# First FFN chunk of each layer: the two tiles' first products by turns, four sums made earlier on VectorE, weight sums in place

## What is computed

```python
def swiglu_ffn(h, w_gu, w_down):
    gate, up = jnp.split(h @ w_gu, 2, axis=-1)
    return (jax.nn.silu(gate) * up) @ w_down
...
x = x + swiglu_ffn(rms_norm(x, ffn_norm[layer]), ffn_w_gu[layer], ffn_w_down[layer])
```

## Time and profile before

| what | value |
|---|---|
| median of 3 runs | 2767.73 us (2766.87 to 2770.54) |
| profiled execution | 2769.94 us, span 2768.1 us |
| TensorE matmul busy | 2699.3 us, 98% of the span |
| VectorE / ScalarE / GpSimd busy | 1355.6 / 826.3 / 1263.7 us |
| chain that ended last | TensorE 91%, VectorE 5%, ScalarE 2% |
| mean granted TensorE clock | 0.994 |

### The profile page before, as it was taken

How to read it: one execution, slowest core, us unless ns; L and a number is a source line. 1 busy time by engine, 2 the same in 40 slices (tenths; PEclk the granted TensorE clock), 3 DMA queues, 4 the chain that set the end, 5 groups by cost and what they waited for, 6 DMA issues and landing times.

```text
span 2768.1 us, 35757 instructions
## 1 busy us (share of the span) xinstructions
PE 2699.3 (98%) x12145; PEld 2236.5 (81%) x12145; DVE 1355.6 (49%) x1866; ACT 826.3 (30%) x1404; POOL 1263.7 (46%) x1215
## 2 busy tenths in 40 slices
PE   7999999999999899999999999999988999999998
PEld 6888888888888788888888788787876888888886
DVE  7423423432334764454545537355577454545555
ACT  4220210120023523333323524324165222222223
POOL 3323323323422555665555444253445555655554
PEclk9999999999999999999999999999999999999999
DMA  4112102111111111111121011111110211111212
GB/s 134 39 30 65 43 31 65 47 31 58 50 35 46 31 58 53 53 45 46 56 64 53 27 55 46 32 58 36 49 50 23 65 53 53 45 45 53 68 50 80
DMA packets 173482, 140.03 MB, mean 51 GB/s; under 512 B 8656, under 2 KB 142928, under 8 KB 173392
## 3 DMA queue, kind: packets, MB, share of 16 engines
q1 hardware_dynamic: 171664, 133.53, 15.8%
q10 hardware_dynamic: 1728, 5.26, 0.5%
HBM read 133.51 MB, written 5.24 MB: 50 GB/s over the span
## 4 chain that ended last, share of the span: by engine, by line
PE 91%; DVE 5%; ACT 2%; issue 1%; POOL 0%; DMA 0%; POOLq 0%; SPq 0%; DVEq 0%; ACTq 0%
PE ps L693 30%; PE ps L696 30%; PE ps L697 30%; PE ps L779 1%; DVE uc L1945 1%; PE ps L897 0%; DVE residual L1601 0%; DVE residual L1858 0%; DVE gate_buf L1950 0%; DVE residual L2016 0%; DVE f_h_lo L1741 0%; DVE h_sum_a L1730 0%; DVE uc L1940 0%; ACT L1470 0%; ACT L1464 0%
## 5 line engine op out<-in xcount | busy, mean ns | idle before, releaser
L530 POOL TENSOR_TENSOR f_w_lo<-f_raw,f_w_hi 128x512 fp32r<-128x512 f32 x262 | 341.1, 1305 | 434.3 <-ACT f_w_hi L1243 434.2
L693 PE MATMUL ps<-f_h_hi,f_w_hi 128*128 128x512 f32 x1232 | 483.0, 392 | 19.5 <-DVE f_h_lo L1730 12.1
L696 PE MATMUL ps<-f_h_lo,f_w_hi 128*128 128x512 f32 x1232 | 481.3, 391 | 0.0
L697 PE MATMUL ps<-f_h_hi,f_w_lo 128*128 128x512 f32 x1232 | 481.0, 390 | 0.0
L490 POOL TENSOR_TENSOR small<-w_raw 128x1 f32<-128x1 f32 x200 | 54.3, 272 | 847.2 <-PE ps L693 832.0
L1858 DVE TENSOR_TENSOR residual<-ps,residual 128x512 f32<-128x512 f32 x352 | 239.3, 691 | 157.7 <-PE ps L697 157.7
L693 PEld LDWEIGHTS ps<-f_h_hi,f_w_hi 128*128 128x128 f32 x1232 | 232.4, 189 | 71.6 <-issue 16.4
L1243 ACT ACTIVATE f_w_hi<-f_raw 128x512 fp32r<-128x512 f32 x262 | 164.1, 628 | 367.3 <-PE ps L697 349.6
L697 PEld LDWEIGHTS ps<-f_h_hi,f_w_lo 128*128 128x128 f32 x1232 | 232.4, 189 | 48.7
L696 PEld LDWEIGHTS ps<-f_h_lo,f_w_hi 128*128 128x128 f32 x1232 | 232.5, 189 | 48.0
L693 PE MATMUL ps<-f_w_hi,f_act_hi 128*128 128x512 f32 x688 | 267.6, 389 | 0.0
(11 more groups left out here) (261 smaller groups left out, 4778.7 us busy)
## 6 DMA issues: line engine op xcount, KB each, us to landing
f_raw<-in_ffn_w_gu SPq DMA_DIRECT2D x176, 256.0 KB, 3.3
w_raw<-in_ret_w_in SPq DMA_DIRECT2D x96, 256.0 KB, 2.8
f_raw<-in_ffn_w_down SPq DMA_DIRECT2D x88, 256.0 KB, 2.7
w_raw<-in_lru_w_in SPq DMA_DIRECT2D x48, 256.0 KB, 2.9
w_raw<-in_ret_w_out SPq DMA_DIRECT2D x32, 256.0 KB, 2.6
w_raw<-in_lru_w_out SPq DMA_DIRECT2D x24, 256.0 KB, 2.6
residual<-in_x SPq DMA_DIRECT2D x8, 512.0 KB, 6.5
out_y<-residual SPq DMA_DIRECT2D x8, 512.0 KB, 2.6
```

Source lines behind the costliest of these rows:

```text
L530: nc.gpsimd.tensor_tensor(lo, src, hi.bitcast(F32), ALU.subtract).then_inc(f_wready, 1)
L693: m = nc.tensor.matmul(o, l_hi, r_hi, start=start, stop=False, skip_group_check=onto)
L696: nc.tensor.matmul(o, l_hi, r_lo, start=False, stop=False, skip_group_check=onto)
L697: return nc.tensor.matmul(o, l_lo, r_hi, start=False, stop=stop, skip_group_check=onto)
```

## The change

The order of the 14 products becomes 0, 4, 1, 2, 3 with tile 0 and tile 1 by turns, then 5, 6 of tile 0 and 5, 6 of tile 1. Products 1, 2, 3 and 5 of tile 0 wait for their activation forms quarter by quarter (`there(k)`) instead of for all four ahead. VectorE makes T3 and T2 straight from Q22's banks, before ScalarE copies them (`fourth` now waits for T2). The six remainders of GpSimd go to VectorE, and T2 and T3 remainders are put between those of Q22. The weight sums of each tile are written over their own inputs, so that those of tile 1 need not wait for tile 0, and the four loads of down weights wait for other units. After the forms, VectorE and ScalarE run new written-out orders of the two tiles' activation work (`first_tiles_up`, `first_chunk`); `first_sum` adds product 1, 2 or 3 to the tile's running sum, `gate_1`, `up_1`, `act_1` make the first half of a tile, `gate_2`, `act_2` the second (with `sigmoid_2` between), `split` the remainders. Transposes 12 to 15 use banks 2, 6, 7, 3 instead of 6, 7, 2, 3.

```diff
-PLACES_FIRST = [(0, 0), (1, 0), (0, 4), (1, 4)] + [(u, p) for u in range(2) for p in (1, 2, 3, 5, 6)]
+PLACES_FIRST = [(u, p) for p in (0, 4, 1, 2, 3) for u in range(2)] + [(u, p) for u in range(2) for p in (5, 6)]
...
+EV_FIRST = [(0, E_T5), (1, E_T5), (0, E_T7), (0, E_T6), (0, E_G1), (0, E_C21), (1, E_T7), (1, E_T6),
+            (0, E_C12), (0, E_G2), (1, E_G1), (1, E_C21), (1, E_C12), (1, E_G2)]
+SUMS_FIRST = [(0, 1), (0, 2), (0, 3), (1, 1), (1, 2), (1, 3), (0, 6), (1, 6)]
...
-HT_BANK = (4, 5, 6, 7, 4, 5, 6, 7, 1, 2, 3, 5, 6, 7, 2, 3)
+HT_BANK = (4, 5, 6, 7, 4, 5, 6, 7, 1, 2, 3, 5, 2, 6, 7, 3)
...
+                        if first:
+
+                            sp.wait_ge(f_wready, units + AT_FIRST[0, (3, 2, 5, 6)[i]] + 1)
...
-                    f_add(one, raws[u][1], raws[u][2], ALU.add)
+                    f_add(f_in_sum(u), raws[u][1], raws[u][2], ALU.add)
...
+                    seen(u, 0)
+                    summed(u, 2)
+                    f_add(raws[u][0], f_in_sum(u), raws[u][0], ALU.subtract)
...
+                    seen(u, 4)
+                    summed(u, 3)
+                    f_add(raws[u][3], raws[u][0], raws[u][3], ALU.subtract)
...
                 sum_3(0)
                 lower(1, 0, raws[1][0])
                 sum_2(0)
+                landed(0, 3)
                 lower(0, 4, raws[0][3])
-                lower(1, 4, raws[1][3])
-                lower(0, 1, one)
-                sum_4(0)
-                lower(0, 2, raws[0][1])
-                for k in FOUR:
-                    form("T3l", H_T3, k, t_b, "T3h")
-                pool.wait_ge(f_summed, sums + 3)
-                lower(0, 3, two)
-                for k in range(2):
-                    form("T2l", H_T2, k, t_a, "T2h")
-                lower(0, 5, raws[0][2])
-                pool.wait_ge(f_summed, sums + 4)
-                lower(0, 6, one)
-                seen(0, 6)
-                seen(0, 3)
                 sum_1(1)
                 sum_3(1)
-                lower(1, 1, one)
                 sum_2(1)
+                landed(1, 3)
+                lower(1, 4, raws[1][3])
+                sum_4(0)
+                lower(0, 1, f_in_sum(0))
+                lower(1, 1, f_in_sum(1))
+                sum_4(1)
+                lower(0, 2, raws[0][1])
                 lower(1, 2, raws[1][1])
-                sum_4(1)
-                lower(1, 3, two)
+                summed(0, 3)
+                lower(0, 3, raws[0][0])
+                summed(1, 3)
+                lower(1, 3, raws[1][0])
+                lower(0, 5, raws[0][2])
+                summed(0, 6)
+                lower(0, 6, raws[0][3])
                 lower(1, 5, raws[1][2])
-                pool.wait_ge(f_summed, sums + 8)
-                lower(1, 6, one)
+                summed(1, 6)
+                lower(1, 6, raws[1][3])
...
                 product(n, 1, 4, AT_FIRST)
-                seen(("T1h", 3), ("T1l", 3))
-                product(n, 0, 1, AT_FIRST)
-                seen(("T3h", 3), ("Q22l", 3), ("T3l", 3))
-                product(n, 0, 2, AT_FIRST)
-                seen(("T2h", 3), ("T2l", 3), ("T2l", 1))
-                product(n, 0, 3, AT_FIRST)
-                seen(("T4h", 3), ("T4l", 3))
+
+                product(n, 0, 1, AT_FIRST, lambda k: seen(("T1h", k), ("T1l", k)))
+                product(n, 1, 1, AT_FIRST)
+                seen(None, ("Q22l", 0))
+                product(n, 0, 2, AT_FIRST, lambda k: seen(("T3h", k), ("T3l", k)))
+                seen(None, ("Q22l", 1))
+                product(n, 1, 2, AT_FIRST)
+                seen(None, ("Q22l", 3))
+                product(n, 0, 3, AT_FIRST, lambda k: seen(("T2h", k), ("T2l", k)))
+                seen(None, ("Q22l", 2))
+                product(n, 1, 3, AT_FIRST)
+                again(n, 0, 5, True)
+                product(n, 0, 5, AT_FIRST, lambda k: seen(("T4h", k), ("T4l", k)))
+                again(n, 0, 6, True)
+                seen(("Q22h", 2))
+                product(n, 0, 6, AT_FIRST)
                 for p in (5, 6):
-                    again(n, 0, p)
-                    product(n, 0, p, AT_FIRST)
-                for p in (1, 2, 3, 5, 6):
-                    again(n, 1, p)
+                    again(n, 1, p, True)
...
-                for k in range(5):
-                    if k < 4:
-                        from_bank(H_hi[:, h_cut(H_Q22, k)], 12 + k)
-                    if k:
-                        from_sum(H_T3, k - 1, t_b, "T3")
+                for k in FOUR:
+                    from_sum(H_T3, k, t_b, "T3")
+                fourth(0)
                 unit(6)
-                for k in FOUR:
-                    from_sum(H_T2, k, t_a, "T2")
+                fourth(1)
+                fourth(3)
+                fourth(2)
                 unit(7)
+                from_sum(H_T2, 0, t_a, "T2")
+                from_sum(H_T2, 1, t_a, "T2")
+                unit(8)
+                from_sum(H_T2, 2, t_a, "T2")
+                from_sum(H_T2, 3, t_a, "T2")
+                unit(9)
+                for u in range(2):
+                    sigmoid_1(c, u, AT_FIRST)
+                unit(10)
                 for k in FOUR:
                     from_sum(H_T4, k, t_a, "T4")
...
+            def first_chunk(layer, behind):
+
+                n = chunk_no(layer, 0)
+                for j in (11, 12):
+                    multiplied(n, j)
+                    w_round_first(n, j)
+                act_round(n, 0, 0)
+                multiplied(n, 13)
+                w_round_first(n, 13)
+                sigmoid_2(n, 0, True)
+                act_round(n, 0, 1)
+                multiplied(n, 14)
+                w_round(n, 14)
+                act_round(n, 1, 0)
+                sigmoid_2(n, 1, True)
+                act_round(n, 1, 1)
+                multiplied(n, 15)
+                w_round(n, 15)
+                behind()
+                for j in (16, 17, 18, 19):
+                    multiplied(n, j)
+                    w_round(n, j)
...
-                    seen("Q22h", k)
+                    seen("q12", k)
                     from_bank(t_b[:, t_cut(k)], 12 + k, t_b[:, t_cut(k)])
+                for k in (0, 1, 3, 2):
+                    t_2(k)
+                plain(H_Q22, 0, 12, "Q22h")
                 for k in FOUR:
-
-                    dve.wait_ge(hn_dve, hn_at(HN_DVE, "T1l", k, layer))
-                    from_bank(t_a[:, t_cut(k)], 12 + k, t_a[:, t_cut(k)])
+                    lower(H_T3, k, t_b, "T3h")
+                plain(H_Q22, 1, 13, "Q22h")
+                plain(H_Q22, 3, 15, "Q22h")
                 for k in FOUR:
-                    plain(H_Q22, k, 12 + k, "Q22h")
-                for k in (2, 3):
                     lower(H_T2, k, t_a, "T2h")
+                plain(H_Q22, 2, 14, "Q22h")
                 t_4(0)
                 t_4(1)
                 for k in FOUR:
+
                     dve.wait_ge(hn_dve, hn_at(HN_DVE, "T4", k, layer))
                     lower(H_T4, k, t_a, "T4h")
+                    if k == 0:
+                        first_sum(layer, 0, E_T5)
                     if k < 2:
                         t_4(k + 2)
...
+                first_sum(layer, 1, E_T5)
+                first_sum(layer, 0, E_T7)
+                first_sum(layer, 0, E_T6)
+                gate_1(0)
+                up_1(0)
+                act_1(0)
+                first_sum(layer, 1, E_T7)
+                first_sum(layer, 1, E_T6)
+                split(0, 0)
+                gate_2(0)
+                act_2(0)
+                gate_1(1)
+                up_1(1)
+                split(0, 1)
+                act_1(1)
+                gate_2(1)
+                split(1, 0)
+                act_2(1)
+                split(1, 1)
```

More of the change, by code:

```diff
@@ L263, in t_cut, with ev_at @@
             return slice(k * 512, (k + 1) * 512)
+        def ev_at(n, u, e, first):
+            return n * F_EV + (EV_FIRST.index((u, e)) if first else 7 * u + e) + 1
         def chunk_no(layer, c):
@@ L567, in first_units @@
                 raws = [[f_in_raw(4 * u + i) for i in range(4)] for u in range(2)]
-                one, two = f_in_sum(0), f_in_sum(1)
                 def landed(u, i):
@@ L577, in seen, with summed @@
                     pool.wait_ge(f_wready, units + AT_FIRST[u, p] + 1)
-                def form(what, form, k, src, hi):
-                    pool.wait_ge(hn_act, hn_at(HN_ACT, hi, k, layer))
-                    nc.gpsimd.tensor_tensor(H_lo[:, h_cut(form, k)], src[:, t_cut(k)],
-                                            H_hi[:, h_cut(form, k)].bitcast(F32), ALU.subtract).then_inc(hn_pool, 1)
+                def summed(u, p):
+                    pool.wait_ge(f_summed, sums + SUMS_FIRST.index((u, p)) + 1)
                 def sum_1(u):
@@ L913, in _, with product @@
             head(HEADS - 1, False, True)
-            def product(n, u, p, at=AT):
+            def product(n, u, p, at=AT, there=lambda k: None):
                 j, form = at[u, p], H_OF[p]
```

(45 more changed lines are left out.)

122 lines of the change are left out of this document (70 added, 52 removed).

## The result

| | before | after |
|---|---|---|
| median of 6 runs each, same chip | 2769.39 us | 2752.53 us |
| lowest to highest | 2766.87 to 2771.33 | 2751.67 to 2753.02 |
| ratio, 95% interval | | 0.9942 [0.9932, 0.9951] |
| profiled execution, its span | 2769.94, 2768.1 | 2752.61, 2750.8 |

A forecast was written before the change was run, and what follows sets the result against it. TensorE bounds the kernel; only its waits and low-clock matmuls, 28.2 us over both layers' first chunks, could be gained. Losses of 7.5 and 8.0 us would remain: gain 12.7, forecast 2755.0 us, range 2747 to 2764.

The forecast's parts named there:

- start of (0,2): Tile 0's product 2, waiting for its first T3 remainder: a wait of 0.5 us in place of 6.2.
- T3's third and fourth quarter: Inside product (0,2): GpSimd's weight remainders meet VectorE's third and fourth T3 remainders, 1.0 us each, a wait of about 1.9 us.
- T4's quarters: Product (0,5), going quarter by quarter behind VectorE's T4 remainders, waits about 0.7 us.
- down's first unit: Before the first down matmul: the unit, behind tile 0's second half on ScalarE's queue, is ready 1.8 us late.
- restarts: First matmul behind each wait takes a little longer: eight times 0.08, 0.6 us.
- down's second unit: Down's second weight unit, held behind tile 1's second half: 0.4 us.
- taken on top: Margin for timing errors and added collisions: layer 0's summed 6.6 us of loss taken as 7.5.
- one collision: VectorE operation with both operands in SBUF, held up while GpSimd subtracts: 1.04 us on the mean.
- A: Rival: the wait before down grows from 1.8 towards 2.9 us and the clock falls there, 2760 us; chance 0.16.
- C: Rival: the wait only moves, all collisions occur and VectorE's chain limits both tiles, 2 us gained, 2766 us; chance 0.10.
- B: Rival: few collisions, a third or so of them, gain some 20 us, 2748 us; chance 0.11.
- D: Rival: slower, the chopped stretch holds the clock down through the ten products to down, 2788 us; chance 0.07.

The follow-up runs named there:

- sums_early: Changed kernel with down's units 14, 15 rounded earlier on ScalarE and two gate_buf first sums moved ahead of T2's remainders on VectorE: 2745.81 us, ratio 0.9916.
- forms_first: Kernel before with one part of the change alone, VectorE making T3 and T2 ahead of ScalarE's copy of Q22: 2768.98 us, ratio 1.0004.
- old_forms: Changed kernel with one part undone, ScalarE again copying Q22 by turns with T3 and VectorE making T3 behind that copy: 2756.04 us, ratio 0.9953.
- pool_forms: Changed kernel with the six remainders (T3 all, T2's first two) back on GpSimd: 2754.44 us, ratio 0.9948.
- wait_mid: Changed kernel with idle ScalarE copies ahead of tile 0's second sigmoid, 1024 columns in layer 0, 2048 in layer 1: 2757.9 us, ratio 0.9960.
- wait_ends: Changed kernel with idle ScalarE copies ahead of tile 0's second sigmoid, 3072 columns in layer 0, 512 in layer 1: 2758.36 us, ratio 0.9962.
- whole_waits: Changed kernel with products 1, 2, 3 and 5 of tile 0 each waiting for all four quarters of their form: 2753.02 us, ratio 0.9946.

## Why the prediction came out right, and where its terms were off

The mechanism held: the wait and the slow matmuls behind it are gone, and the wait before down is the largest left. The sum held less well than 2755.0 for 2752.53 looks: the stages gained 15.4 us for a forecast of 12.7, and the six runs' median of the kernel before, 1.7 us above the one that the forecast started from, hid a part of the difference. Term by term, layer 0; what TensorE was late is the trace's wait plus 0.16 us, since the trace counts a matmul as 0.39 us long and the next could start 0.23 us after it:

| term | predicted | measured |
|---|---|---|
| start of (0,2) | 0.5 | 0.35 + 0.16 = 0.5 |
| T3's third and fourth quarter | 1.9 | 0 |
| T2's fourth quarter | 0 | 0.67 + 0.16 = 0.8 |
| T4's quarters | 0.7 | 0.15 + 0.27 + 2 x 0.16 = 0.7 |
| (0,6) | 0.5 | 0.4 |
| weights | 0.2 | 0.18 + 0.16 = 0.3, and 0.16 at (1,2) |
| down's first unit | 1.8 | 1.39 + 0.16 = 1.55 |
| restarts | 0.6 | 7 x 0.08 = 0.6 |
| down's second unit (behind the stretch) | 0.4 | 953.26 - 953.02 = 0.2, 0.5 with what follows |
| taken on top | 0.9 | |

Without the last two rows the prediction has 6.2 us, the measured terms without (1,2) have 4.9, and the stretch lost 47.24 - 41.6 = 5.6. Of the 0.7 us between, 0.2 are two more restarts, behind the groups of transposes. The rest is mostly in starts that the view gives no wait for: 0.16 us at (1,2), 0.09 at T4's fourth quarter (936.00), and the restarts behind these two and behind 927.10. Down to chunk 1, layer 0 lost 6.1 us where I took 7.5 with the margin of 0.9, and layer 1 lost 6.7 for 8.0: 2.7 us in all. The margin was not needed; 1.9 at T3 was too much, and nothing at T2 too little.

T4's term came out for times that both were off: T4's first remainder was ready at 931.99, 0.7 us sooner than 934.6 in this trace's time (1.9 us earlier than that of the earlier trace rows), and (0,5) started about 0.85 us sooner too. Behind a wait that the view puts down to ScalarE's rounding (933.94, 935.14), VectorE's remainder was the last to come: it ended 0.15 us ahead of the start.

*The term that was mis-sized* is that of T3: "which meet the third and fourth T3 remainder: 1.0 us each", with a wait of 1.9 us inside product (0,2). It measured 0. I had let the two engines take turns from the moment GpSimd arrives. In the trace VectorE's running series of four went through and GpSimd's subtraction was held for 1.35 us, which cost TensorE 0.16 us at (1,2). VectorE was held at T2's remainders instead, by the second and third of GpSimd's subtractions and by the next unit: three times, where I had counted three and a half up to there, two of them at T3. TensorE had 2.4 us of slack there, nearly a product, so 3.25 us of holding cost it 0.8 at T2's fourth quarter; VectorE makes T4 behind it, so T4's remainders came later too. sums_early shows the same from the other side: with GpSimd's work unchanged, VectorE is held twice and not three times. Why a GpSimd operation sometimes waits out a whole series and sometimes gets the next turn is not settled: in the changed kernel it came 0.4 us after a VectorE operation had started and was passed over twice, while the one that began at 924.67, with T2's first remainder just begun, had the next turn.

*The size of one collision.* I took 1.04 us, a mean over two. Held remainders cost (5.74 - 2.49) / 3 = 1.08 us here. So the size was right, and nearly the count; the place, and with it what reached TensorE, was not. The Trainium skill, page "SBUF — State Buffer", section "Who interferes with whom", gives a whole GpSimd instruction (1.29 us here) as what can be lost; the trace agrees in kind and stays below it.

*The rivals.* A did not come: the wait before down shrank instead of growing, 1.39 us. Its mechanism is real: a wait of 2.33 us at that very place does lower the clock, so 0.9 us more of tile 0's chain would have brought it, at 1.2 us a layer beside the wait, not 2.6. C was refuted by the stretches, though forms_first shows it at work where the tiles are not interleaved. B was right for T3's remainders alone; by the stages its gain of some 20 us is further off than the forecast's. D was refuted: with seven short waits the clock of the stretch is 1.00. The Trainium skill, page "TensorE: Matmul & The Clock Gate", section "A second HAM failure mode: psum-queue depth-cycling", names short idles between bank-cycling groups as a danger; waits of 0.15 to 1.39 us and even 2.29 us between such groups left 2.4 GHz standing here, so no run shows it.

*The two parts of the gain.* The prediction costed the forms' order only inside the whole. The pair forms_first and old_forms shows what that hid: worth nothing in the kernel before, 2.8 us by the stages in the changed one.

## What to carry to other kernels

When one wait is long enough to lower the clock, putting another tile's work into it can earn the wait and the slow matmuls behind it (the stretches are 7.5 and 8.9 us shorter here, with the other parts of the change); shortening it alone can earn nothing, because the next late chain takes over and lowers the clock again. Behind such a change look for what an in-order queue holds up in front of the first consumer: an exchange of two places on ScalarE gave 4.1 us by the stages. Where VectorE and GpSimd both work on operands in SBUF, put VectorE's operations that read PSUM where GpSimd works: 1.8 us here by the stages.

## What the runs showed of the hardware

Which waits lowered TensorE's clock in this chunk, over the kernels run: 2.04 (pool_forms, layer 0), 2.33 (wait_mid), 2.44 (old_forms, both layers; in layer 1 one of 0.76 us followed before the clock fell), 3.30 (wait_mid) and 4.32 us (wait_ends) did, as did 3.35 to 4.41 in forms_first and 6.07 and 6.04 before. 1.39 and 1.40 (after), 1.77 (before), 1.90 (wait_ends), 2.02 (forms_first), 2.05 (pool_forms, layer 1), 2.27 and 2.29 us (whole_waits) did not. So from 2.0 to 2.3 us the length of the wait doesn't decide alone, and no run here isolates what else does: the 2.04 and the 2.05 stand at the same product of one kernel, with waits of 0.25 and 0.32 us ahead of both. The slow time behind a fall was short: 6 to 13 matmuls at 0.43 us apart for 0.23, 3 to 6 us.

The exclusion between VectorE and GpSimd is not a strict turn-taking: a GpSimd subtraction of 1.29 us took 2.64 behind a VectorE series that went on past it, and again 2.63 in sums_early, while VectorE lost nothing. Of VectorE's 128x512 operations with an operand in PSUM, 26 to 40 met GpSimd in each kernel around the two stretches, and each took 0.68 to 0.75 us, as it does without GpSimd; of those with two operands in SBUF the held ones took up to 1.84 for 0.68.
